# A two-layer hybrid decoder trunk on 8 cores: more pooling steps beside the second head pair, a later memory norm, head results copied out of PSUM by VectorE, first norms without GpSimd, and output transfers of several channel blocks

## The reference, cut to what matters

```python
D_MODEL, SEQ, DEPTH, MEM_LEN = 1024, 2048, 2, 256
for l in range(DEPTH):
    h = rmsnorm(x, norm_mix_g[l])
    proj = h @ w_in[l]                    # pooling input, q, k, v, forget gates, SGU input, 3 branch gates
    y_a = pool_mixer(a, pool_w[l], pool_scale[l]) @ w_branch_a[l]      # trailing means over 2, 4, 8, 16
    y_b = forgetting_attention(q, k, v, logf) @ w_branch_b[l]          # 8 heads of 64, causal
    y_c = spatial_gating(gelu(...), ...) @ w_branch_c[l]
    x = x + (gates_a * y_a + gates_b * y_b + gates_c * y_c) @ w_out[l]
    hx, hm = rmsnorm(x, norm_xattn_g[l]), rmsnorm(mem, norm_mem_g[l])
    x = x + softmax((hx @ w_xq[l]) @ xk.T / 16) @ xv @ w_xo[l]         # 4 heads, 256 memory tokens, xk, xv from hm @ w_xkv[l]
    x = x + square(relu(rmsnorm(x, norm_ffn_g[l]) @ w_ff1[l])) @ w_ff2[l]
return rmsnorm(x, final_norm_g)
```

## Time and profile before

| | |
|---|---|
| three runs | 2342.43, 2346.14, 2504.66 us, median 2346.14 |
| profiled execution | 2363.35 us |
| its span, slowest core (core 2) | 2361.8 us |
| spans of cores 0 to 3 and 4 to 7 | 2354.6 to 2361.8 us and 2333.1 to 2336.5 us |
| mean granted TensorE clock | 0.985 to 0.988 and 0.997 |
| head pairs of layer 0, of layer 1 | about 74 to 316 us, 1232 to 1467 us |
| last matmul ends, span ends | about 2350.4 us, 2361.8 us |

### The profile page before, as it was taken

One profiled execution on the slowest core, in us unless ns is written; L12 is line 12 of the kernel. 1 busy time (PEld: TensorE's weight loads), 2 busy tenths in 40 slices (PEclk: granted clock), 3 DMA queues, 4 the chain that ended last, 5 costly groups with the idle time before them and its releaser, 6 DMA issues.

```text
span 2361.8 us, 37792 instructions; the slowest of 8 cores (2333.1 to 2361.8 us)
## 1 busy us (share of the span) xinstructions
PE 2290.1 (97%) x13762; PEld 1146.7 (49%) x13984; DVE 1159.4 (49%) x1827; ACT 950.1 (40%) x1460; POOL 280.8 (12%) x284
## 2 busy tenths in 40 slices
PE   7999999999999999999999999999999999999997
PEld 3565654444444444444456566444444444444444
DVE  5565444444546434343574644444444564334345
ACT  5786742224543111202347867222354330302023
POOL 6102200002101000000210131000111110000000
PEclk9999999999999999999999999999999999999998
DMA  8500943336504332221412039333252134322013
GB/s 189 78 11 2 139 95 36 36 36 99 72 1 54 45 45 36 36 41 50 104 50 29 11 55 159 53 39 36 46 89 36 19 48 51 43 38 27 1 36 108
DMA packets 170293, 128.87 MB, mean 55 GB/s; under 512 B 6912, under 2 KB 143488, under 8 KB 170112
## 3 DMA queue, kind: packets, MB, share of 16 engines
q0 software_dynamic: 139680, 80.92, 27.7%
q1 hardware_dynamic: 30432, 45.51, 6.8%
HBM read 190.14 MB, written 16.78 MB: 88 GB/s over the span
## 4 chain that ended last, share of the span: by engine, by line
PE 91%; ACT 3%; issue 2%; DVE 2%; DMA 1%; POOL 1%; SPq 0%; DVEq 0%; ACTq 0%; POOLq 0%
PE ps L490 91%; ACT pb L441 1%; DMA wide<-w_xo 1%; DMA x<-xT 0%; DVE T L454 0%; DVE x L454 0%; ACT T L441 0%; DVE qT L461 0%; POOL A L447 0%; POOL sB L447 0%; DVE kT L466 0%; ACT L441 0%; ACT P L441 0%; DVE A L454 0%; POOL sq L447 0%
## 5 line engine op out<-in xcount | busy, mean ns | idle before, releaser
L490 PE MATMUL ps<-A,wsl 128*128 128x512 bf16 x3495 | 797.8, 382 | 7.6 <-DVE qT L461 2.3
L490 PEld LDWEIGHTS ps<-A,wsl 128*128 128x128 bf16 x3584 | 350.4, 98 | 424.0 <-issue 29.4
L441 ACT ACTIVATE T<-ps 128x512 f32<-128x512 f32 x224 | 133.7, 597 | 589.8 <-PE ps L490 588.4
L447 DVE TENSOR_TENSOR x<-ps,x 128x512 f32<-128x512 f32 (+2 forms) x336 | 220.4, 664 | 303.3 <-PE ps L490 302.9
L490 PE MATMUL ps<-hid,wsl 128*128 128x512 bf16 x1506 | 331.8, 380 | 1.6
L441 ACT ACTIVATE pb<-ps 128x1024 bf16<-128x1024 f32 (+1 forms) x320 | 275.8, 897 | 63.4 <-PE ps L490 62.6
L490 PEld LDWEIGHTS ps<-hid,wsl 128*128 128x128 bf16 x1536 | 150.5, 98 | 181.9 <-issue 2.9
L454 DVE SCALAR_TENSOR_TENSOR T<-T,ps 128x512 f32<-128x512 f32 x160 | 107.1, 685 | 261.3 <-PE ps L490 218.2
L447 DVE TENSOR_TENSOR hid<-T 128x512 bf16<-128x512 f32 x192 | 132.9, 692 | 206.9 <-ACT T L441 206.9
L441 ACT ACTIVATE T<-ps,halfb 128x512 f32<-128x512 f32 x128 | 88.0, 687 | 247.8 <-PE ps L490 247.8
L454 DVE SCALAR_TENSOR_TENSOR A<-x,vecs,rstd 128x512 bf16<-128x512 f32 x186 | 134.7, 794 | 21.8 <-ACT rstd L441 21.8
(11 more groups left out here) (140 smaller groups left out, 2394.5 us busy)
## 6 DMA issues: line engine op xcount, KB each, us to landing
wsl<-w_ff POOLq DMA_DIRECT2D x52, 512.0 KB, 5.8
x<-xT SPq DMA_DIRECT2D x64, 256.0 KB
wsl<-w_in POOLq DMA_DIRECT2D x30, 512.0 KB, 10.8
wsl<-w_xkv POOLq DMA_DIRECT2D x16, 512.0 KB, 7.5
xsave<-x SPq DMA_DIRECT2D x32, 256.0 KB
x<-xsave SPq DMA_DIRECT2D x32, 256.0 KB
wsq<-w_qkv POOLq DMA_DIRECT2D x24, 256.0 KB, 6.3
w<-w_ff POOLq DMA_DIRECT2D x12, 512.0 KB, 10.1
```

The source lines that it names most:

```text
L441: P.add("act", [lambda h: h.activation(out=o, in_=i_, func=func, scale=sc, bias=bi)], [out], [in_] + more, 175 + 0.833 * size(out) + 90 * ...
L447: P.add(eng, [lambda h: h.tensor_tensor(out=o, in0=a, in1=b, op=op)], [out], [in0, in1], cost)
L490: fns.append(lambda h, o=o, l_=l_, r_=r_, start=start, stop=stop, kw=kw: h.matmul(o, lhsT=l_, rhs=r_, start=start, stop=stop, **kw))
```

## The change

The change has six parts. (1) `merge` beside pair 1 gets pooling steps 0 to 8 instead of 0 to 4, beside pair 2 the other 8 instead of 12. (2) `mem_norm` and `scale_v` are spread among the filler of pair 2 instead of standing at its head. (3) `turn` copies its bank into `ao` with `copy` (DVE) instead of `act`. (4) The first norms have no `aside`: all eight products are DVE's. (5) The planner counts 500 ns instead of 60 for a transfer issued by SP. (6) The outputs go out in transfers of 4 blocks, those of the very last 128 tokens in transfers of 2.

```diff
@@ dma
-            P.add(eng, ..., writes, reads, 900 if eng == "pool" else 60, lat=slack,
+            P.add(eng, ..., writes, reads, 900 if eng == "pool" else 500, lat=slack,
@@ turn, in attention
-                        act(ao[:, hc, Qi * TT:(Qi + 1) * TT], ps[:, b, :], AF.Identity)
+                        copy(ao[:, hc, Qi * TT:(Qi + 1) * TT], ps[:, b, :])
@@ norm0
-                return [lambda: norm_tile(lambda dc: xsl(dc, t), vb, lambda dc: Asl(dc, t), bank=fb(), aside=(2, 5) if t else ())] if l == 0 else []
+                return [lambda: norm_tile(lambda dc: xsl(dc, t), vb, lambda dc: Asl(dc, t), bank=fb())] if l == 0 else []
@@ the merges
-            merge(attention(1), both(allqkv(2, 2), gate_v + gate_u[:0] + pool_[:5]) + rows(2))
+            merge(attention(1), both(allqkv(2, 2), gate_v + gate_u[:0] + pool_[:9]) + rows(2))
...
-            merge(attention(2), gate_u[0:1] + [mem_norm, scale_v_] + both(allqkv(3), pool_[5:]) + rows(3))
+            merge(attention(2), gate_u[0:1] + both([mem_norm, scale_v_] + allqkv(3), pool_[9:]) + rows(3))
@@ after
-                    for dc in range(8):
-                        dma("sp", outT[dc, :, t * TT + c0:t * TT + c0 + w], part(dc).ap, [], [part(dc)], 512 * w)
+                    n_ = 8 if w < TT and c0 + w == TT else 4
+                    for d0 in range(0, 8, 8 // (n_ // 2)):
+                        d1 = d0 + 8 // (n_ // 2)
+                        v = xt[t][:, d0:d1, c0:c0 + w]
+                        dma("sp", outT[d0:d1, :, t * TT + c0:t * TT + c0 + w].rearrange("d p c -> p d c"), v.ap, [], [v],
+                            512 * w * (d1 - d0))
```

More of the change, by code:

```diff
@@ L476, in dma @@
         def dma(eng, out, in_, writes, reads, nbytes, group=None, slack=0):
-            P.add(eng, [lambda h: h.dma_start(out=out, in_=in_)], writes, reads, 900 if eng == "pool" else 60, lat=slack,
+            P.add(eng, [lambda h: h.dma_start(out=out, in_=in_)], writes, reads, 900 if eng == "pool" else 500, lat=slack,
                   dma=True, group=group, nbytes=nbytes)
```

## The result

The changed kernel takes 2330.48 us (median of 4 runs, 2329.20 to 2331.26), 0.9941 of the kernel before, 95% interval 0.9917 to 0.9965, which is 13.8 us less than the 2344.29 us between the two runs of 2342.43 and 2346.14. In three further sessions it stood at 2326.1 to 2328.3 us against 2340.2 to 2340.6 for the kernel before: 12.0 to 14.2 us less. (A kernel on all cores is now and then disturbed by a lower clock on a whole die; the medians given from here on are of the undisturbed runs.) The forecast was 2335, range 2323 to 2349. The time lies in the range, but the gain is larger than the −11 us of the sum, and the largest single part of it, some 6.5 us (e6), belongs to a step that the sum had put at nothing.

The account below looks back on a forecast made before the run. PE was taken as the bound, busy 2290.1 of 2361.8 us, so only its idle time could be won. Start −2.5, pairs −4 and end −4.5 make −11 us, from 2346.14 to 2335 us, range 2323 to 2349.

Parts of the forecast that it names:

- the sum: Whole kernel: start −2.5, pairs −4, end −4.5, together −11 us, taken from 2346.14 to give 2335 us.
- the pooling's: Pairs 1 and 2: four pooling steps go from pair 2 to pair 1, merely changing place; net 0, ±1.5 a layer.
- the relief of ACT: Pairs: moving 32 `ao` copies off ACT removes a third of PE's waits for exponentials; −5 us, bounds 0 and −14.4.
- The end: After DVE's last product: SP's output issues are the bound, and larger transfers win −4.5 us, bounds −5.3 and 0.
- The start: Start of layer 0: with all eight products on DVE, most of PE's 2.71 us wait for POOL goes; −2.5 us.
- The constants: Start of layer 0: four conversions now stand ahead of DVE's copies of `qf`; cost 0, at most +1 us.
- The sum of the pairs: Pairs of both layers: lighter ACT −5, waits for DVE +1, memory norm and pooling 0; net −4 us.
- The sign that was to prove it: Pairs: PE's wait for `pb`, the exponentials, would be 8 to 10 us instead of 14.4.
- The stricter sign: Pairs: if PE's waits for `pb` and for DVE tiles together are still above 17 us, ACT's relief was nothing.
- the relief of ACT is worth nothing: Pairs: PE would wait for the next exponential anyway, so only start and end gain; 2340 us, chance 0.12.
- The planner's 500 ns: SP's transfers: the new price changes no duration and moves reloads of `x` a little, needed only far later; 0.
- The rival with DVE as the bound: Filler banks beside the pairs: `turn` holds one until DVE comes; slower above 0.35 us a turn; 2353 us, chance 0.12.

Follow-up runs that it names:

- e6: The changed kernel with five pooling steps beside pair 1 and twelve beside pair 2 again: 2333.00 us, −7.6 us against the kernel before.
- e3: The changed kernel with the `ao` copies back on ACT: 2326.94 us, −13.3 us against the kernel before.
- e8: The changed kernel with the planner's cost of an SP transfer back at 60 ns: 2328.43 us, −12.2 us against the kernel before.
- e9: The changed kernel with seven pooling steps beside pair 1 in place of nine: 2336.96 us, −4.9 us against the kernel before.
- e14: The changed kernel with eight pooling steps beside pair 1 in place of nine: 2333.01 us, −6.3 us against the kernel before.
- e17: The changed kernel with ten pooling steps beside pair 1 in place of nine: 2335.32 us, −4.9 us against the kernel before.

## Why the prediction was right and wrong

The step that failed is the pooling's: "four steps go from pair 2 to pair 1 ... merely change place ... Net 0, ±1.5 a layer". Measured are −1.8 and −2.1 us a layer, and with the falls of the clock 6.5 us of the time (e6). The second is the relief of ACT, put at −5 and measured at −0.2 by the stages (e3). That the two errors nearly cancel in the sum is luck.

*The end* (−4.5): right. −4.7 by the stage, SP's price near the lower bound, the landing 3.05 us behind the last product in place of 3.3. Only the 290 GB/s of full transfer engines were too low: they moved 344 at a share of 0.97. *The start* (−2.5): right in what was removed and about 0.5 too large, since the wait for v's weights came in its place; the working named `DVE A` as the gap that might take over and not the weights. *The constants*: 0, right; `qf` starts at 26.16 (before 26.51) and waits for PE.

*The sum of the pairs* (−4) is about right and its two terms are wrong. "I take a third: −5" for ACT's relief: e3 shows 0.2 us. The sign that was to prove it, PE's wait for `pb` at 8 to 10 us, was fulfilled, but it is fulfilled with `ao` on ACT too (10.0). The stricter sign, "if these together are still above 17, the relief was nothing", told the truth: 9.5 for `pb` and 3.1 + 2.5 + 1.3 + 0.7 for `qT`, `on`, `ao` and `kT` are 17.1. The rival "the relief of ACT is worth nothing" was right about the relief, though its time of 2340 was not, and rows 6 show no more than that an `ao` once stood ahead of an exponential. The pooling's step looked at cover in proportion, gaps of 2.8 and 5.5 us, and the 5.5 are 3.65 on a core with a complete trace and no fall. Beside them in rows 3 stood a clock of 0.97, from which the prediction drew nothing; it only set the lower clock of cores 0 to 3 aside as a matter of that execution. In this window the 0.97 is a fall of the same kind. Core 2 of the kernel before:

```profile
195.00:197.00 2.00, 1.82 (x23) 1.61 (x24) 0.54 (x1) 0.54 (x2) 0.00 (x0) 0.67 0.03 8
197.00:199.00 2.00, 1.78 (x9) 0.82 (x8) 0.00 (x0) 1.93 (x3) 0.00 (x0) 0.50 0.02 4
199.00:201.00 2.00, 2.00 (x17) 1.03 (x16) 0.25 (x1) 0.60 (x1) 0.00 (x0) 0.98 0.00 0
```

They are short of 0.66 + 1.00 + 0.04 = 1.70 us of clock, which is 0.025 of the 67. The other die's cores 4, 5 and 6, whose mean clock was 0.997, show it as well, once each.

Of the 1.9 us between five and nine steps in layer 0, PE's idle time shows 0.7 (235.71 − 224.71 against 233.83 − 223.57). The other 1.1 lies inside its busy time, with the same number of matmuls. One group is 1.0 us longer: 320 of them, of 128 columns, are recorded as 0.22 us long and follow each other closer than that, so a short wait between two vanishes in the modelled end of the first:

```profile
L490 PE MATMUL ps<-wsq,A 128*128 128x128 bf16 x320 | 20.6, 219 | 0.9 <-DVE qT L461 0.9
```

```profile
L490 PE MATMUL ps<-wsq,A 128*128 128x128 bf16 x320 | 21.6, 219 | 1.0 <-DVE qT L461 0.9
```

(First the changed kernel, then e6, both core 1, layer 0's pairs.) That the small waits are there is read from the equal counts and the longer stage; that it is these waits and nothing else was not shown.

*The planner's 500 ns* (0): the durations are unchanged, as said, but without it three cores fell in pair 1, and the median was 1.9 us higher (e8, with runs that overlap). "They move SP's reloads of `x` a little" was taken for harmless because they are needed late; what moved was the company of other steps.

*The rival with DVE as the bound*: did not happen. DVE was at 78% in pair 1, PE's waits for `qT` fell from 3.9 to 3.1 us, and for `ao` it waited 1.3. Two signs that the sum would be wrong did appear, a wait for a weight (1.8 us) and one for `ao`; neither points at the step that failed.

*The chances.* "A measurement of this kernel tells no less than about 2% from no change" is wrong: the intervals are ±0.1 to ±0.3%, and most stages agree to 0.1 us. A change of 0.6% was plain to see. The bound of 72 us was too high as well, since lacking records counted as idle (55 to 58). *The anchor* of 2346.14 was 5.5 us above the median of later sessions. The number 2335 therefore came out 4.5 us above the 2330.48, though the sum, −11, lies near the −11 of the stages without a fall.

What stays open: why one packing is good and the next bad can't be told from the count. In e8, e9 and e14 the falls in pair 1 stand behind a table load at the turn of a row; that the norm's chain or a filler bank that is held does the same at the start of pair 2 was argued and not shown. No rule came out that would have found nine. And why on one core the clock falls at a place and on its neighbour, with the same list, it does not.

## What to carry to other kernels

Moving work between two stages with gaps is not always a mere change of place: look for the places in each stage where PE has only small matmuls with short waits between them, and ask what stands beside these before and after the move. When the time is that of the slowest core, an event that strikes only some of the cores can cost nearly its full price (2.6 of the 6.5 us of e6, by the account above), so cut the clock column into windows of 2 us and look at every core; and before idle time is taken for a bound, compare the counts of matmuls and weight loads. And a tuned count in front of a planner (5, 7, 8, 9, 10, 13 steps gave −7.6, −4.9, −6.3, −12 to −14, −4.9 and −4.2 us) has to be tried number by number; the trend of two of them says nothing.

## What the runs showed of the hardware

The granted clock fell to 1.2 GHz on core 5 of e6 at 189.2, after PE had been busy for 1.70 of the 2.00 us from 186 and 0.76 of the 1.20 from 188, and the fall was worth 1.7 us of clock. It came on some cores and not on others that ran the same instructions at the same place. In e9, e14 and e17 some falls lasted twice as long (core 7 of e14: 0.50 from 166.5 to 173.3). At the end of all kernels it is at 0.50 when PE has no matmuls left, so rows behind the last matmul say nothing of it. A stage of 233 us repeats from core to core and execution to execution: in four profiles of the changed kernel layer 1's pairs took 232.52 to 232.60 us on 31 of 32 cores, layer 0's 233.75 to 234.00 on 27. And an output transfer of 256 or 512 rows costs SP about as much to issue as one of 128: 0.37 us, and 0.49 in the mean of the last two, against 0.47 in the earlier trace rows.
